# Decode samples' NSA on four column tiles of the PE array: compression, scores and value products re-laid

## The chip, the cores and the metric

The program runs on one core of a Trainium2 chip. A core has the matrix engine TensorE (PE in the profile; its weight loads are PEld), VectorE (DVE), ScalarE (ACT), GpSimd (POOL), and SyncE (SP), which here issues nearly all DMAs. They run side by side and wait for each other on semaphores. The metric is the device time of one execution in microseconds (us); lower is better.

## The reference, cut to what matters

The reference is one step of a hybrid decoder layer over a prompt of 1024 tokens and 8 decode samples with one new token each. The change is in the samples' NSA attention (`NS` = 8 samples, `NH` = 8 heads of `HD` = 64 in 2 kv groups, a cache of 1024 rows in 8 pages of 128):

```
kc, vc = compress(cached k, w_k), compress(cached v, w_v)   # blocks of 32 rows, weighted sum: 32 blocks per sample
p_c = softmax(q . kc);  o_c = p_c . vc                      # compressed branch
imp = sum of p_c over the group's 4 heads, pairs of blocks  # importance of 16 selection blocks of 64 rows
idx = top_k(imp, 16) of the 17 blocks (16 old, 1 new)       # so one old block is left out
o_s = softmax(q . k[idx]) . v[idx]                          # selected branch, 1024 rows
o_w = softmax(q . k_win) . v_win                            # window branch, 512 rows
out = g0 * o_c + g1 * o_s + g2 * o_w
```

Beside it the layer merges two mixers: `sigmoid(h W_a) * (ya W_pa) + sigmoid(h W_b) * (yb W_pb)` over 1032 tokens.

## The kernel before, in words

The program has long stages one after the other: adaLN, input projections, mLSTM, prompt attention, then the **merge stage** (from 850 to 1195 us of the trace), output rows, up projection, down projection. The samples' NSA has no stage of its own: it is laid into the merge stage. That stage has 24 units u. A unit of PE has one or two gate chains (8 f32 matmuls of 344 columns, stationary 128x128, line L2623), then the chains of ya and yb (4 matmuls each), eight together. Behind the gate chain stands `samples_pe(2u+1)`, behind the y chains `samples_pe(2u+2)`. `samples_dve` and `samples_act` have their calls at the same places on DVE and ACT. So the order on every engine is fixed in the code, by the number n = 2u+1 or 2u+2.

What stands there for sample b, before:

- n = 2b+3 (b = 0 to 7): first `scores` of sample b-1 (L2601 to L2603: the queries of all samples, zero but for one, as 64 stationary columns, against 1024 selected keys, 512 window keys and 32 compressed keys, accumulated over the samples in PSUM), then the transposes of b's 8 key pages (L2541), which DVE and ACT copy to SBUF.
- n = 2b+4: 4 transposes of the window keys (L2547), then compression: keys with the page stationary and 4 moving columns (L2554), values with a 32-column block pattern stationary (L2557). GpSimd must have multiplied the pages by the compression weights before (L1059), and does so as soon as all of b's keys are in.
- n = 19 to 24: softmax of the compressed branch, importance (L2562), mask, softmax of the others, transposes of the probabilities (L2566 to L2571).
- n = 25: products for the new row (L2575, L2576) and the compressed values (L2578), into one PSUM tile for all samples.
- n = 25 to 32: sample n-25's values: 12 pages stationary (128x128), 8 probabilities moving (L2585, L2588).
- n = 32: a closing matmul of zeros (L2592); DVE copies the result into ybT, which the unit u = 16 needs.

An f32 matmul stands twice in the trace (x16 is eight of the program).

**SP's queue** is one list, in this order: keys 0, merge weights 1, keys 1, merge weights 2, keys 2, keys 3, three outputs, merge weights 3, keys 4, keys 5, merge weights 4, keys 6, keys 7, merge weights 5, values 0 to 3, merge weights 6, merge weights 7, values 4 to 7, merge weights 8 and so on. One set of keys is 8 pages, for each a page number read from a table (L796), one DMA for the compressed rows (L798) and one for the selected keys (L800), then one for the window (L802). It goes into one of 2 slots and waits until the sample two before has been compressed. Values have 4 slots (L811 waits, L813 and L815 load); values 4 to 7 wait for the products of values 0 to 3. Merge weights (L835) have 2 slots; set m is for the units 2m and 2m+1 (m up to 7), and waits until the units of set m-2 are done.

Of the kernel before, what the change touches and what calls it, by code (L numbers as in the profile page):

```python
# [8 lines left out]
ALU = mybir.AluOpType  # L9
# [6 lines left out]
P = 128  # L16
# [4 lines left out]
NS = 8  # L21
# [40 lines left out]
def constants():  # L62
# [5 lines left out]
    parts["pick"] = (((np.arange(P)[:, None] % 32) == np.arange(16)[None, :]) & (np.arange(16)[None, :] < 9)) * 1.0  # L68
# [62 lines left out]
def build(nc, t, outs):  # L131
# [3 lines left out]
    with ExitStack() as ctx:  # L135
# [239 lines left out]
        vcs = take(NCMP, NS, NKV * HD)  # L375
        Qall, Qpad = take(P, NS, NH), take(P, NS, NH)
        knT = take(P, 2, NS)
        ckT = take(P, NCMP)
        assert at <= NT * MIX, at
        SR = NS * NH  # L380
        at = at_nsa
        pT, wT = take(P, PAST), take(P, WIN)
        PTs, PTw = pT[:, 0:512].unsqueeze(1), pT[:, 512:1024]
        Ssl, Swn = take(SR, PAST + NS), take(SR, WIN + NS)
# [19 lines left out]
        Scm, pcm = take(SR, NCMP), take(SR, NCMP)  # L404
# [98 lines left out]
        def up_lo(place, k):  # L503
# [36 lines left out]
        s_sps, s_Qall, s_soft, s_softm, s_softe, s_sPT, s_sPTe = (  # L540
            sem(n) for n in ("samples_ps", "Q_all", "soft", "soft_max", "soft_exp", "sPT_ps", "sPT"))
# [3 lines left out]
        SP_Q, SP_Y, SP_IMP, SP_O = 1, 2, 3, 4  # L545
# [561 lines left out]
        def _(act):  # L1107
# [136 lines left out]
            def samples_act(n):  # L1244
# [21 lines left out]
                if n == 19:  # L1266
                    for turn, x, j in ((1, Scm, 0), (2, Swn, 2)):
                        act.wait_ge(s_softm, turn)
                        nc.scalar.activation(x, x, ACT.Exp, bias=small[:, j:j + 1], accum_out=small[:, 4 + j:5 + j]).then_inc(s_softe, 1)
# [3 lines left out]
                if n == 24:  # L1273
                    act.wait_ge(s_sPT, 1)
                    nc.scalar.activation(PTs[:, 0, :], ps[:, 4, :], ACT.Copy).then_inc(s_sPTe, 1)

# [158 lines left out]
        def _(dve):  # L1435
# [356 lines left out]

            def samples_dve(n):
# [11 lines left out]
                if n == 1:  # L1805
# [6 lines left out]
                    dve.sem_inc(s_Qall, 1)  # L1812
# [19 lines left out]
                if 3 <= n <= 18 and n % 2 == 0:  # L1832
                    b = (n - 4) // 2
                    dve.wait_ge(s_pgps, 2 * b + 2)
                    nc.vector.tensor_copy(ckT, ps[:, 5, 0:NCMP])
                    nc.vector.tensor_copy(vcs[:, b, :], ps[0:NCMP, 5, 64:64 + P])
                    nc.vector.tensor_tensor(Qpad, Qall, cst("onehot")[:, b * NS:(b + 1) * NS].unsqueeze(2).to_broadcast([P, NS, NH]),
                                            ALU.mult).then_inc(s_pgd, 1)
# [32 lines left out]
                if n == 19:  # L1871
                    dve.wait_ge(s_soft, 1)
                    nc.vector.tensor_copy(Scm, ps[0:SR, 3, 64:64 + NCMP])
                    step(nc.vector.tensor_copy(Swn[:, 0:WIN], ps[0:SR, 2, :]))
# [3 lines left out]
                    nc.vector.tensor_reduce(small[:, 0:1], Scm, AX.X, ALU.max, negate=True).then_inc(s_softm, 1)  # L1878
                    nc.vector.tensor_reduce(small[:, 2:3], Swn, AX.X, ALU.max, negate=True).then_inc(s_softm, 1)
                    step(nc.vector.memset(zrow, 0.0))  # L1880
                if n == 20:
                    dve.wait_ge(s_softe, 1)
# [24 lines left out]
                if n == 24:  # L1907
                    dve.wait_ge(s_sPT, 1)
                    nc.vector.tensor_copy(PTw[:, 0:256], ps[:, 5, 0:256])
                    nc.vector.tensor_copy(PTw[0:NCMP, 256:320], ps[0:NCMP, 5, 256:320])  # L1910
                    nc.vector.tensor_copy(PTw[0:NS, 320:448], ps[0:NS, 5, 320:448]).then_inc(s_sPTe, 1)
                if n == 32:
                    dve.wait_ge(s_sps, SP_O)
# [256 lines left out]
        def _(pe):  # L2170
# [345 lines left out]
            def samples_pe(n):  # L2516
# [8 lines left out]
                if n == 3:  # L2525
                    pe.wait_ge(s_Qall, 1)
# [16 lines left out]
                if 3 <= n <= 18 and n % 2 == 0:  # L2543
# [16 lines left out]
                if n == 22:  # L2560
                    pe.wait_ge(s_soft, 2)
                    nc.tensor.matmul(ps[0:SR, 4, 0:NCMP], cst("same_group", SR), pcm, start=True, stop=True).then_inc(s_sps, 1)  # L2562
                if n == 24:
                    pe.wait_ge(s_soft, 3)
# [4 lines left out]
                    nc.tensor.transpose(ps[0:NCMP, 5, 256:320], Scm, ident[0:SR, 0:SR])  # L2569
                    nc.tensor.transpose(ps[0:NS, 5, 320:384], Ssl[:, PAST:], ident[0:SR, 0:SR])  # L2570
                    nc.tensor.transpose(ps[0:NS, 5, 384:448], Swn[:, WIN:], ident[0:SR, 0:SR]).then_inc(s_sPT, 1)  # L2571
                if n == 25:
# [4 lines left out]
                    for b in range(NS):  # L2577
                        nc.tensor.matmul(ps[:, 0, b * NH:(b + 1) * NH], vcs[:, b, :], PTw[0:NCMP, 256 + b * NH:256 + (b + 1) * NH],  # L2578
                                         start=False, stop=False, skip_group_check=True)
                if 25 <= n <= 32:  # L2580
                    b, v = n - 25, (n - 25) % 4
                    pe.wait_ge(*values_landed(b))
                    out = ps[:, 0, b * NH:(b + 1) * NH]
                    for j in range(NPAGE):
                        nc.tensor.matmul(out, pv_slc[v][:, j, :], PTs[:, 0, j * SR + b * NH:j * SR + (b + 1) * NH],  # L2585
                                         start=False, stop=False, skip_group_check=True)
                    for j in range(WIN // P):
                        ins = nc.tensor.matmul(out, pv_win[v][:, j, :], PTw[:, j * SR + b * NH:j * SR + (b + 1) * NH],  # L2588
                                               start=False, stop=False, skip_group_check=True)
                    ins.then_inc(s_free, 1)  # L2590
                if n == 32:
                    nc.tensor.matmul(ps[:, 0, 0:SR], ones[0:1, :], zrow[:, 0:SR], start=False, stop=True).then_inc(s_sps, 1)  # L2592

            def scores(b):

                first, last = b == 0, b == NS - 1
                pe.wait_ge(s_pga, 2 * b + 2)
                pe.wait_ge(s_pgd, 2 * b + 2)
                Q2 = Qpad.rearrange("p b h -> p (b h)")
# [204 lines left out]
```

## Time and profile before

| | us |
|---|---|
| median of 3 runs | 2087.64 |
| lowest, highest run | 2083.59, 2087.82 |
| span of the profiled execution (first to last instruction) | 2085.8 |
| PE busy in it | 2017.6 (97%) |
| DVE, ACT, POOL busy | 816.0, 517.7, 371.4 |
| mean granted TensorE clock | 0.983 |

The profiled execution has no time of its own beside its span; the median of the runs lies 1.84 us above that span. All places in the trace are in us from the span's start. A row of the timeline has the start, the length until the last of the group ends, engine, line, operation, tiles, shapes and how many. Matmuls overlap, so what a group costs is the distance from its start to the start of the row behind it, not its length.

### The profile page before, as it was taken

How to read it: one execution, taken by the hardware profiler on the slowest of the kernel's cores; microseconds unless marked ns; L12 is line 12 of the kernel's file. 1: busy time of each engine (PE TensorE's matmuls, PEld its weight loads, DVE VectorE, ACT ScalarE, POOL GpSimd, SP SyncE). 2: the span in 40 equal slices, each digit the busy share in tenths (PEclk: the TensorE clock that was granted, in tenths of full speed). 3: DMA queues.
4: the chain of work that ended last, by engine and by line, in shares of the span. 5: the costliest groups of instructions: out<-in, count | busy, mean ns of one | idle time of the engine just before them, and what ended most of it. 6: DMA issues, size and time to landing. Idle time of an engine off the chain costs nothing.

```text
span 2085.8 us, 28720 instructions
## 1 busy us (share of the span) xinstructions
PE 2017.6 (97%) x11391; PEld 1601.0 (77%) x11391; DVE 816.0 (39%) x1535; ACT 517.7 (25%) x942; POOL 371.4 (18%) x440
## 2 busy tenths in 40 slices
PE   6999999989999998999999999999999999999998
PEld 3589877775666665666676677999999999988876
DVE  2444333475656566622201257511211111235344
ACT  2322200133344444211200046411111111123232
POOL 0000111222222223222000043000000000145553
PEclk9999999989999999999989999999999999999999
DMA  9443001032000000454324355221121112235453
GB/s 362 142 152 102 21 30 34 1 90 81 11 11 11 11 11 11 135 159 139 104 81 110 87 180 179 62 62 41 41 59 43 41 44 58 91 121 169 144 192 112
DMA packets 172077, 184.38 MB, mean 88 GB/s; under 512 B 9925, under 2 KB 142253, under 8 KB 171502
## 3 DMA queue, kind: packets, MB, share of 16 engines
q1 hardware_dynamic: 171950, 182.59, 27.8%
q8 instruction: 91, 1.49, 0.3%
q14 instruction: 36, 0.29, 0.0%
HBM read 170.22 MB, written 16.53 MB: 90 GB/s over the span
## 4 chain that ended last, share of the span: by engine, by line
PE 89%; DVE 3%; DMA 2%; ACT 2%; issue 1%; SPq 1%; POOL 1%; ACTq 0%; POOLq 0%; DVEq 0%
PE ps L2722 23%; PE ps L2623 11%; PE ps L2226 8%; PE ps L2493 5%; PE ps L2665 5%; PE ps L2247 5%; PE ps L2667 5%; PE ps L2666 5%; PE ps L2444 3%; PE ps L2483 3%; PE ps L2461 3%; PE ps L2186 1%; PE ps L2557 1%; PE ps L2585 1%; PE ps L2601 1%
## 5 line engine op out<-in xcount | busy, mean ns | idle before, releaser
L2722 PE MATMUL ps<-h_hi,wup_hi 128*128 128x344 f32 x1008 | 322.4, 320 | 3.5 <-DVE arena L2076 3.5
L2722 PE MATMUL ps<-h_lo,wup_hi 128*128 128x344 f32 x1008 | 323.1, 321 | 0.0
L2722 PE MATMUL ps<-h_hi,wup_lo 128*128 128x344 f32 x1008 | 322.5, 320 | 0.0
L1082 POOL CAST ra_hi<-arena 128x384 fp32r<-128x384 f32 (+1 forms) x90 | 48.5, 539 | 848.2 <-PE ps L2722 453.1
L2226 PE MATMUL ps<-arena,hT 128*128 128x261 f32 (+2 forms) x768 | 193.5, 406 | 3.4 <-ACT hT L1137 2.5
L2665 PE MATMUL ps<-rw_hi,ra_hi 128*128 128x512 f32 x480 | 191.8, 400 | 5.1 <-DVE rw_lo L1924 5.1
L2722 PEld LDWEIGHTS ps<-h_hi,wup_hi 128*128 128x128 f32 x1008 | 189.5, 188 | 4.0 <-issue 2.6
L2722 PEld LDWEIGHTS ps<-h_lo,wup_hi 128*128 128x128 f32 x1008 | 189.6, 188 | 0.0
L2722 PEld LDWEIGHTS ps<-h_hi,wup_lo 128*128 128x128 f32 x1008 | 189.5, 188 | 0.0
L2667 PE MATMUL ps<-rw_lo,ra_hi 128*128 128x512 f32 x480 | 189.4, 395 | 0.0
L2666 PE MATMUL ps<-rw_hi,ra_lo 128*128 128x512 f32 x480 | 188.7, 393 | 0.0
L2226 PEld LDWEIGHTS ps<-arena,hT 128*128 128x128 f32 x768 | 143.1, 190 | 42.6 <-issue 7.4
L1051 POOL TENSOR_SCALAR arena<-arena 128x640 f32<-128x640 f32 (+7 forms) x128 | 99.9, 781 | 287.4 <-DVE arena L1774 287.4
L1924 DVE TENSOR_TENSOR rw_lo<-hT,rw_hi 128x1024 fp32r<-128x1024 f32 x65 | 90.1, 1391 | 143.6 <-ACT rw_hi L1281 143.6
L1214 ACT ACTIVATE arena<-ps,arena 128x640 f32<-128x640 f32 (+7 forms) x128 | 89.7, 700 | 186.8 <-DVE arena L1754 185.2
L2493 PE MATMUL ps<-hT,xn 128*128 128x344 f32 x336 | 128.0, 498 | 3.1 <-ACT arena L1238 2.4
L1088 POOL TENSOR_TENSOR ra_lo<-arena,ra_hi 128x384 fp32r<-128x384 f32 (+1 forms) x90 | 125.2, 1391 | 4.8
L2623 PE MATMUL ps<-hT,arena 128*128 128x344 f32 x400 | 123.2, 463 | 0.0
L2623 PE MATMUL ps<-arena 128*128 128x344 f32 x352 | 112.3, 474 | 0.7 <-ACT arena L1289 0.5
L2665 PEld LDWEIGHTS ps<-rw_hi,ra_hi 128*128 128x128 f32 x480 | 90.9, 189 | 28.2 <-issue 7.5
L1281 ACT ACTIVATE rw_hi<-hT 128x1024 fp32r<-128x1024 f32 x65 | 68.7, 1060 | 175.6 <-DMA hT<-in_w_down 175.6
L2667 PEld LDWEIGHTS ps<-rw_lo,ra_hi 128*128 128x128 f32 x480 | 90.8, 189 | 21.0
(429 smaller groups left out, 2923.9 us busy)
## 6 DMA issues: line engine op xcount, KB each, us to landing
hT<-in_w_down SPq DMA_DIRECT2D x65, 512.0 KB, 3.3
arena<-in_w_ada SPq DMA_DIRECT2D x12, 2048.0 KB, 8.1
arena<-in_w_up SPq DMA_DIRECT2D x42, 512.0 KB, 4.7
arena<-in_w_out SPq DMA_DIRECT2D x24, 512.0 KB, 4.1
arena<-in_w_in SPq DMA_DIRECT2D x17, 512.0 KB, 4.4
arena<-in_cache_cmp_kv SPq DMA_DIRECT2D x64, 128.0 KB, 2.0
arena<-in_cache_slc_kv SPq DMA_DIRECT2D x128, 64.0 KB, 1.9
arena<-in_w_in SPq DMA_DIRECT2D x4, 1544.0 KB, 12.9
```

What stands on the lines that cost most here:

```text
L1051: nc.gpsimd.tensor_scalar(pbuf[u % 3][:, 0:nb * P], pbuf[u % 3][:, 0:nb * P], rec[:, u % 4:u % 4 + 1], gts[:, i, col:col + 1], ALU.mult, A ...
L1088: nc.gpsimd.tensor_tensor(lo[:, 0:n], src[:, k, cols], hi[:, 0:n], ALU.subtract).then_inc(s_ra, 1)
L1214: nc.scalar.activation(pbuf[u % 3][:, 0:n], sp_[:, 512 - n // 2:512 + n // 2], ACT.Exp, bias=nmx[:, u % 4:u % 4 + 1], accum_out=rsum[:, u ...
L1924: nc.vector.tensor_tensor(rw_lo[rnd][at][:, :], rw_from(rnd, step), rw_hi[rnd][at][:, :], ALU.subtract).then_inc(s_rlo, 1)
L2226: ins = nc.tensor.matmul(ps[:, bank, 0:width], hT[:, k, n * P:(n + 1) * P], w[:, k, 0:width], start=(k == 0), stop=(k == KD - 1))
L2247: ins = nc.tensor.matmul(ps[:, mix_bank(j, n), 0:PA], h[:, k, :], w[:, k, :], start=(k == 0 and x == 0), stop=(k == KD - 1 and x == 2))
L2493: ins = nc.tensor.matmul(ps[:, 7, 0:TG], wfill[m % 2][:, k, :], hT[:, k, q * TG:(q + 1) * TG], start=(k == 0), stop=(k == KD - 1))
L2623: ins = nc.tensor.matmul(ps[:, bank, 0:TG], w[:, k, :], src[:, k, q * TG:(q + 1) * TG], start=(k == 0), stop=(k == kn - 1))
L2665: nc.tensor.matmul(out, ra_hi[rnd][a][:, rows], rw_hi[rnd][w][:, cols], start=first, stop=False)
L2666: nc.tensor.matmul(out, ra_lo[rnd][a][:, rows], rw_hi[rnd][w][:, cols], start=False, stop=False)
L2667: ins = nc.tensor.matmul(out, ra_hi[rnd][a][:, rows], rw_lo[rnd][w][:, cols], start=False, stop=last)
L2722: ins = nc.tensor.matmul(ps[:, bank, 0:TG], w(place, k0 + k), h[:, k, toks], start=(k == 0 and j == 0), stop=(k == KD - 1 and j == 2))
```

## The change

Compression (n = 2b+4): one matmul gives keys and values. The 32-column block pattern is stationary, and the weighted rows (128 keys, 128 values) are 256 moving columns. Page 2q+r goes to column tile q, that is PSUM partitions 32q to 32q+31; four samples accumulate in one PSUM region, which is copied once per four samples, and its key half transposed by PE (n = 12 and 19).

Scores: the stationary operand is the queries of four samples (32 columns), and the 1536 keys are four pieces of 384, one for each column tile, accumulated over four samples in PSUM bank b // 4. DVE and ACT bring them into the softmax layout (32 rows per four samples) at n = 13 and 19. Scores on compressed keys are one matmul for four samples (`cmp_scores`), with a mask for those of other samples (`cmp_masked`); the compressed softmax is now 64x128 instead of 64x32. DVE takes the block mask onto the copy in SBUF and not from PSUM.

Values: the probabilities of four samples (32 columns) are stationary, the pages of 128 columns move, page 4r+q in column tile q. At the end (new n = 33, behind the gate chain of u = 16) the result (2 copies of 128x512) is turned by 8 matmuls with the page sum `pick`, and added to the new row's and the compressed products. The wait of u = 16 for ybT moves from before both y chains to before the second.

```diff
@@ samples_pe
                 if 3 <= n <= 18 and n % 2 == 0:
...
-                    for j in range(NPAGE):
-                        nc.tensor.matmul(ps[:, 5, 4 * j:4 * j + 4], pg_cmp[s][:, j, 0:P], cst("block")[:, 28:32],
-                                         start=True, stop=True)
-                    for j in range(NPAGE):
-                        ins = nc.tensor.matmul(ps[0:NCMP, 5, 64:64 + P], cst("block")[:, 28 - 4 * j:60 - 4 * j],
-                                               pg_cmp[s][:, j, P:2 * P], start=(j == 0), stop=(j == NPAGE - 1))
+                    if b == 4:
+                        pe.wait_ge(s_qk, QK_CMP[0])
+                        nc.tensor.transpose(ps[:, 5, 0:P], kcv[0][:, 0:P], ident)
+                    if b == 5:
+                        cmp_scores(0, 5, P)
+                    for r in range(2):
+                        at = 8 * (b % 4) + 4 * r
+                        for q in range(4):
+                            ins = nc.tensor.matmul(ps[32 * q:32 * q + 32, 2, b // 4 * 256:b // 4 * 256 + 256],
+                                                   cst("block")[:, 28 - at:60 - at], pg_cmp[s][:, 2 * q + r, :],
+                                                   start=(b % 4 == 0 and r == 0), stop=(b % 4 == 3 and r == 1))
                     ins.then_inc(s_pgps, 1)
+                if n == 19:
+                    pe.wait_ge(s_qk, QK_CMP[1])
+                    nc.tensor.transpose(ps[:, 5, 0:P], kcv[1][:, 0:P], ident).then_inc(s_sps, 1)
+                if n == 20:
+                    pe.wait_ge(s_qk, QK_KT)
+                    cmp_scores(1, 4, 0).then_inc(s_sps, 1)
...
-                    for b in range(NS):
-                        nc.tensor.matmul(ps[:, 0, b * NH:(b + 1) * NH], vcs[:, b, :], PTw[0:NCMP, 256 + b * NH:256 + (b + 1) * NH],
+                    for g in range(2):
+                        nc.tensor.matmul(ps[:, 0, g * 32:(g + 1) * 32], kcv[g][:, P:2 * P], PTw[:, 256 + g * 32:256 + (g + 1) * 32],
                                          start=False, stop=False, skip_group_check=True)
                 if 25 <= n <= 32:
...
-                    for j in range(NPAGE):
-                        nc.tensor.matmul(out, pv_slc[v][:, j, :], PTs[:, 0, j * SR + b * NH:j * SR + (b + 1) * NH],
-                                         start=False, stop=False, skip_group_check=True)
-                    for j in range(WIN // P):
-                        ins = nc.tensor.matmul(out, pv_win[v][:, j, :], PTw[:, j * SR + b * NH:j * SR + (b + 1) * NH],
-                                               start=False, stop=False, skip_group_check=True)
+                    for r in range(3):
+                        for q in range(4):
+                            j = 4 * r + q
+                            w, v_ = (PTs[:, 0, :], pv_slc[v][:, j, :]) if r < 2 else (PTw, pv_win[v][:, q, :])
+                            at = (j if r < 2 else q) * SR + b // 4 * 32
+                            ins = nc.tensor.matmul(ps[32 * q:32 * q + 32, 1 + b // 4, b % 4 * P:(b % 4 + 1) * P], w[:, at:at + 32], v_,
+                                                   start=(r == 0), stop=(r == 2))
                     ins.then_inc(s_free, 1)
-                if n == 32:
+                if n == 33:
+                    pe.wait_ge(s_pga, 2 * NS + 2)
+                    pe.wait_ge(s_pgd, 2 * NS + 1)
+                    for b in range(NS):
+                        nc.tensor.matmul(ps[:, 0, b * NH:(b + 1) * NH], Obuf[:, b // 4, b % 4 * P:(b % 4 + 1) * P],
+                                         cst("pick")[:, b % 4 * NH:(b % 4 + 1) * NH], start=False, stop=False, skip_group_check=True)
@@ scores
-                for j in range(2):
-                    nc.tensor.matmul(ps[0:SR, j, :], Q2, pT[:, j * 512:(j + 1) * 512], start=first, stop=last)
-                nc.tensor.matmul(ps[0:SR, 2, :], Q2, wT, start=first, stop=last)
-                nc.tensor.matmul(ps[0:SR, 3, 64:64 + NCMP], Q2, ckT, start=first, stop=last).then_inc(s_free, 1)
+                for q in range(4):
+                    ins = nc.tensor.matmul(ps[32 * q:32 * q + 32, b // 4, 0:KCH], Qpad.rearrange("p b h -> p (b h)"),
+                                           KT[:, q * KCH:(q + 1) * KCH], start=(b % 4 == 0), stop=(b % 4 == 3))
+                ins.then_inc(s_free, 1)
@@ samples_dve, n == 22
-                    step(nc.vector.tensor_reduce(imp, ps[0:SR, 4, 0:NCMP].rearrange("p (k r) -> p k r", r=2), AX.X, ALU.add))
+                    step(nc.vector.tensor_reduce(pcm[:, 0:64], ps[0:SR, 4, 0:P].rearrange("p (k r) -> p k r", r=2), AX.X, ALU.add))
+                    step(nc.vector.tensor_reduce(imp.rearrange("p (q k) -> p q k", q=4),
+                                                 pcm[:, 0:64].rearrange("p (q b k) -> p q k b", q=4, b=4), AX.X, ALU.add))
...
-                    for j in range(2):
-                        ins = nc.vector.tensor_tensor(Ssl[:, j * 512:(j + 1) * 512].rearrange("p (k c) -> p k c", c=SEL),
-                                                      ps[0:SR, j, :].rearrange("p (k c) -> p k c", c=SEL),
-                                                      msk[:, j * 8:(j + 1) * 8].unsqueeze(2).to_broadcast([SR, 8, SEL]), ALU.add)
-                    step(ins)
+                    S3 = Ssl[:, 0:PAST].rearrange("p (k c) -> p k c", c=SEL)
+                    step(nc.vector.tensor_tensor(S3, S3, msk.unsqueeze(2).to_broadcast([SR, 16, SEL]), ALU.add))
```

On PE, one sample's part of the merge stage before, from its scores to the gate chain behind its successor's compression (each row: line of its kernel, operation, tiles, output partitions x columns, how many):

```order
L2601 MATMUL ps<-arena 64x512 x2
L2602 MATMUL ps<-arena 64x512
L2603 MATMUL ps<-arena 64x32
L2541 MATMUL ps<-const,arena 128x128 x8
L2623 MATMUL ps<-arena 128x344 x8
L2547 MATMUL ps<-const,arena 128x128 x4
L2554 MATMUL ps<-const,arena 128x4 x8
L2557 MATMUL ps<-arena,const 32x128 x8
L2623 MATMUL ps<-hT,arena 128x344 x8
```

The same stretch on PE in the changed kernel:

```order
L2654 MATMUL ps<-arena 32x384 x4
L2579 MATMUL ps<-const,arena 128x128 x8
L2678 MATMUL ps<-arena 128x344 x8
L2585 MATMUL ps<-const,arena 128x128 x4
L2600 MATMUL ps<-arena,const 32x256 x8
L2678 MATMUL ps<-hT,arena 128x344 x8
```

Four score matmuls became four of 32 partitions, and the sixteen of the compression eight; chains and transposes stand where they stood.

On PE, n = 25 and the first two samples' values before:

```order
L2575 MATMUL ps<-arena 128x64
L2576 MATMUL ps<-arena 128x64
L2578 MATMUL ps<-arena 128x8 x8
L2585 MATMUL ps<-arena 128x8 x8
L2588 MATMUL ps<-arena 128x8 x4
L2623 MATMUL ps<-arena 128x344 x8
L2585 MATMUL ps<-arena 128x8 x8
L2588 MATMUL ps<-arena 128x8 x4
```

And in the changed kernel:

```order
L2625 MATMUL ps<-arena 128x64
L2626 MATMUL ps<-arena 128x64
L2628 MATMUL ps<-arena 128x32 x2
L2638 MATMUL ps<-arena 32x128 x12
L2678 MATMUL ps<-arena 128x344 x8
L2638 MATMUL ps<-arena 32x128 x12
```

The count per sample stays twelve, with 128 moving columns in place of 8 and a quarter of the output partitions. The instructions of SP and GpSimd are the same in both kernels, in the same order.

## Rows read from the trace of the kernel before

**Rows 1.** Value part: length, busy of PE, PEld, DVE, ACT, POOL, clock, DMA share.

```profile
1033.40:1114.20 80.80, 80.80 (x377) 60.82 (x375) 7.07 (x16) 3.88 (x7) 0.00 (x0) 0.87 0.29 76
```

**Rows 2.** Waits of PE, 850 to 1200 us: total, times, longest.

```profile
PE ps L2541 <- DMA arena<-in_cache_win_kv: 1.2, 1, 1.2
```

**Rows 3.** Timeline of PE, one sample's cycle of the key part.

```profile
953.07 1.93 PE L2601 MATMUL ps<-arena 128*64 128x512 f32 x4
...
955.88 1.09 PE L2541 MATMUL ps<-const,arena 128*128 128x128 f32 x8
...
961.88 1.85 PE L2554 MATMUL ps<-const,arena 128*128 128x4 f32 x16
963.65 1.94 PE L2557 MATMUL ps<-arena,const 128*32 128x128 f32 x16
965.52 4.89 PE L2623 MATMUL ps<-hT,arena 128*128 128x344 f32 x16
970.34 1.07 PE L2601 MATMUL ps<-arena 128*64 128x512 f32 x2
```

**Rows 4.** Timeline of PE, matmuls with 32 stationary columns on four column tiles.

```profile
30.48 1.92 PE L2186 MATMUL ps<-arena 128*32 128x512 f32 x16
...
132.29 1.50 PE L2232 MATMUL ps<-arena,hT 128*32 128x386 f32 x16
133.73 0.44 PE L2247 MATMUL ps<-mw_hi,mh_hi 128*128 128x386 f32 x1
```

**Rows 5.** Timeline of POOL: it starts when a sample's keys have landed.

```profile
867.08 4.68 POOL L1059 TENSOR_TENSOR arena<-arena 128x1024 f32<-128x1024 f32 x2 [20.65 <-DMA arena<-in_cache_win_kv]
883.21 4.68 POOL L1059 TENSOR_TENSOR arena<-arena 128x1024 f32<-128x1024 f32 x2 [11.44 <-DMA arena<-in_cache_win_kv]
...
932.30 4.66 POOL L1059 TENSOR_TENSOR arena<-arena 128x1024 f32<-128x1024 f32 x2 [14.68 <-DMA arena<-in_cache_win_kv]
...
982.87 4.66 POOL L1059 TENSOR_TENSOR arena<-arena 128x1024 f32<-128x1024 f32 x2 [13.39 <-DMA arena<-in_cache_win_kv]
```

**Rows 6.** Timeline of SP's queue: one set of keys, its first and last issue.

```profile
949.06 0.36 SPq L798 DMA_DIRECT2D arena<-in_cache_cmp_kv  x1
...
961.99 0.43 SPq L802 DMA_DIRECT2D arena<-in_cache_win_kv  x1
```

**Rows 7.** Waits of SP's queue for the samples, 850 to 1020 us.

```profile
SPq L796 <- PE ps L2557: 6.1, 3, 3.2
SPq L811 <- PE ps L2557: 1.0, 1, 1.0
```

**Rows 8.** Timeline of SP: values 0's first issue, and merge weights 6.

```profile
983.60 8.16 SPq L813 DMA_DIRECT2D arena<-in_cache_slc_kv  x8
...
1021.62 0.50 SPq L835 DMA_DIRECT2D arena<-in_w_in  x1
...
1022.79 0.51 SPq L835 DMA_DIRECT2D arena<-in_w_proj_b  x1
```

**Rows 9.** DMA issues by line: count, KB each, us to landing.

```profile
arena<-in_w_proj_b SPq DMA_DIRECT2D x15, 256.0 KB, 5.2
```

**Rows 10.** Timeline of PE, value part.

```profile
1033.46 4.89 PE L2623 MATMUL ps<-hT,arena 128*128 128x344 f32 x16
1038.28 0.43 PE L2575 MATMUL ps<-arena 8*128 8x64 f32 x2
...
1040.60 3.16 PE L2585 MATMUL ps<-arena 128*128 128x8 f32 x16
...
1060.31 1.85 PE L2585 MATMUL ps<-arena 128*128 128x8 f32 x16
...
1062.91 4.87 PE L2623 MATMUL ps<-arena 128*128 128x344 f32 x16
```

**Rows 11.** Windows in the value part, columns as in rows 1.

```profile
1041.20:1051.20 10.00, 10.00 (x31) 7.64 (x31) 0.51 (x1) 0.00 (x0) 0.00 (x0) 0.50 0.09 26
1082.10:1085.40 3.30, 3.30 (x8) 2.12 (x8) 0.00 (x0) 0.00 (x0) 0.00 (x0) 0.50 0.22 64
```

More of the change, by code:

```diff
@@ L374, in build @@
         at = 21568
-        vcs = take(NCMP, NS, NKV * HD)
-        Qall, Qpad = take(P, NS, NH), take(P, NS, NH)
+        kcv = [take(P, 2 * NKV * HD) for _ in range(2)]
+        ckT = [take(P, P) for _ in range(2)]
+        SR = NS * NH
+        Scm, pcm = take(SR, P), take(SR, P)
+        Qall, Qpad = take(P, NS, NH), take(P, 4, NH)
         knT = take(P, 2, NS)
-        ckT = take(P, NCMP)
         assert at <= NT * MIX, at
-        SR = NS * NH
         at = at_nsa
-        pT, wT = take(P, PAST), take(P, WIN)
+        KCH = (PAST + WIN) // 4
+        KT = take(P, PAST + WIN)
+        pT, wT = KT[:, 0:PAST], KT[:, PAST:]
         PTs, PTw = pT[:, 0:512].unsqueeze(1), pT[:, 512:1024]
+        Obuf = room(at, 2, 4 * P)
         Ssl, Swn = take(SR, PAST + NS), take(SR, WIN + NS)
@@ L1265, in samples_act @@
                     nc.scalar.activation(hg[:, 9:10], hg[:, 9:10], ACT.Sqrt).then_inc(s_shd, 1)
[L1266 to L1269, printed above, removed]
+                if n in (13, 19):
+                    g = int(n == 19)
+                    act.wait_ge(s_free, 4 * g + 4)
+                    for q in range(2):
+                        ins = nc.scalar.activation(Ssl[32 * g:32 * g + 32, q * KCH:(q + 1) * KCH], ps[32 * q:32 * q + 32, g, 0:KCH], ACT.Copy)
+                    if g:
+                        ins.then_inc(s_pga, 1)
+                if n in (19, 20):
+                    turn, x, j = ((1, Swn, 2), (2, Scm, 0))[n - 19]
+                    act.wait_ge(s_softm, turn)
+                    nc.scalar.activation(x, x, ACT.Exp, bias=small[:, j:j + 1], accum_out=small[:, 4 + j:5 + j]).then_inc(s_softe, 1)
                 if n == 22:
@@ L1275, in samples_act @@
                     nc.scalar.activation(PTs[:, 0, :], ps[:, 4, :], ACT.Copy).then_inc(s_sPTe, 1)
+                if n == 32:
+                    act.wait_ge(s_free, NS + 4)
+                    nc.scalar.activation(Obuf[:, 0, :], ps[:, 1, :], ACT.Copy).then_inc(s_pga, 1)
             def rows_hi(rnd, step):
@@ L1790, in _, with cmp_masked @@
                     att_max(n + 2)
+            def cmp_masked(g, bank, at):
+                rows = slice(32 * g, 32 * g + 32)
+                own = cst("own_new")[rows, 4 * g:4 * g + 4].unsqueeze(1).unsqueeze(3).to_broadcast([32, 4, 4, 8])
+                return nc.vector.tensor_tensor(Scm[rows, :].rearrange("p (q b c) -> p q b c", q=4, b=4),
+                                               ps[rows, bank, at:at + P].rearrange("p (q b c) -> p q b c", q=4, b=4), own, ALU.add)
             def samples_dve(n):
@@ L1877, in samples_dve @@
                     step(nc.vector.memset(Swn[:, 0:1], NEG))
-                    nc.vector.tensor_reduce(small[:, 0:1], Scm, AX.X, ALU.max, negate=True).then_inc(s_softm, 1)
                     nc.vector.tensor_reduce(small[:, 2:3], Swn, AX.X, ALU.max, negate=True).then_inc(s_softm, 1)
+                    dve.wait_ge(s_sps, SP_KT)
+                    nc.vector.tensor_copy(ckT[1], ps[:, 5, 0:P]).then_inc(s_qk, 1)
                     step(nc.vector.memset(zrow, 0.0))
                 if n == 20:
-                    dve.wait_ge(s_softe, 1)
+                    dve.wait_ge(s_sps, SP_CMP)
+                    step(cmp_masked(1, 4, 0))
+                    nc.vector.tensor_reduce(small[:, 0:1], Scm, AX.X, ALU.max, negate=True).then_inc(s_softm, 1)
+                if n == 21:
+                    dve.wait_ge(s_softe, 2)
                     step(nc.vector.reciprocal(small[:, 8:9], small[:, 4:5]))
@@ L2604, in scores, with cmp_scores @@
-                if last:
-                    pe.wait_ge(s_free, NS)
-                    pe.sem_inc(s_soft, 1)
+                for q in range(4):
+                    ins = nc.tensor.matmul(ps[32 * q:32 * q + 32, b // 4, 0:KCH], Qpad.rearrange("p b h -> p (b h)"),
+                                           KT[:, q * KCH:(q + 1) * KCH], start=(b % 4 == 0), stop=(b % 4 == 3))
+                ins.then_inc(s_free, 1)
+            def cmp_scores(g, bank, at):
+                return nc.tensor.matmul(ps[32 * g:32 * g + 32, bank, at:at + P], Qall[:, 4 * g:4 * g + 4, :].rearrange("p b h -> p (b h)"),
+                                        ckT[g], start=True, stop=True)
```

61 lines of the change are left out of this document (35 added, 26 removed).

## Prediction

> **What bounds the kernel now.** I read the page first: PE is busy 97% of the span and the chain of waits is 89% PE, so PE's time counts wherever it does not wait. The samples' NSA lies between 865 and 1114 us. The list of PE's waits there has one wait for data, 1.2 us for the first keys [rows 2]; the timeline shows everything else back to back. So now each microsecond of the samples' matmuls is paid in full. The second view is SP's queue and the landing of its loads, because a shorter PE can ask for data sooner than SP brings it. I think that this view decides the size.
>
> **What PE alone would save.** Distances between starts, in the steady cycle of one sample [rows 3], 17.27 us long: scores 953.07 to 955.88, 2.81 us; compression 961.88 to 965.52, 3.64; the rest (two chains, twelve transposes) 10.8.
> What 32 columns on four column tiles cost, the trace shows in another stage: sixteen matmuls of 512 columns show 1.92 us together, and four of 512 on one tile show 1.93 [rows 3, 4]. So four tiles run side by side, 0.43 us for a group of four. Sixteen of 386 columns take 1.44 us to the next start (132.29 to 133.73 [rows 4]), four groups of 0.32 and some 0.12 to change back. For changing into such a group I put 0.09 more, an estimate a little under the 0.12 of changing back; before scores the kernel already changes (to 64 columns), so it counts only for compression and values. This gives:
> - scores, 8 of 384 columns: 2 x 0.32 + 0.12 = 0.76, saves 2.05;
> - compression, 16 of 256 columns: 4 x 0.22 + 0.12 + 0.09 = 1.09, saves 2.55;
> - so a cycle of 17.27 - 4.60 = 12.67 us;
> - values: now 1060.31 to 1062.91, 2.60 us per sample [rows 10]. New: 24 of 128 columns in 6 groups. The nearest row is L2557, also 32 stationary and 128 moving but on one tile: 1.87 us for 16, 0.117 each [rows 3]. Side by side 6 x 0.117 + 0.2 = 0.90, saves 1.70, x 8 = 13.6. One after the other it would be 24 x 0.117 + 0.2 = 3.0, a loss of 0.4. I take the first, because rows 4 are the same four tiles.
>
> A rule of the Trainium skill speaks against this: in "TensorE: Matmul & The Clock Gate", Part 3 (packing small matmuls), weight loads overlap running matmuls only when the row group differs, and column tiles share it. By that each group would pay a load of some 0.11 us too, 6 x 0.11 x 8 = 5.3 us for the values, and the time would be 2059. Rows 4 disagree: 0.43 us per group is just the streaming of 512 columns and leaves no room for a load.
>
> **The keys: SP takes most of it back.** One set of keys takes 12.9 us from first to last issue [rows 6], some 0.8 us for the page number of the next set stands between, and every second set has three DMAs of merge weights behind it, about 1.7 us. So SP needs some 14.5 us per sample on average, against PE's new 12.67. How much of SP's time before was waiting for PE? In the whole key part 6.1 us, three times, and none before keys 5 [rows 7]. So the landings of keys 0 to 4 do not move at all, and those of keys 7 move by at most 6.1. POOL shows the landings: 867.08, 883.21, 932.30 (keys 4), 982.87 (keys 7) [rows 5]. After: PE would be ready for keys 1 at 880.2 (867.08, a cycle, and 0.4 for a small mLSTM product) and gets them at 883.2; it gets keys 4 at 932.3; keys 7 at 982.87 - 6.1 = 976.8. Before, PE took keys 7 at 973.15 + 17.27 = 990.4. PE alone would have come there at 956.2, so 20 of its microseconds turn into waits of 1 to 6 us ahead of the transposes. From the transposes to the start of compression it is 6.00 us (955.88 to 961.88 [rows 3]), with compression 7.1: the last compression ends at 983.9 instead of 1000.05. GpSimd's 4.68 us from landing [rows 5] are within the 6.0 us before compression needs them, so they stay hidden. Behind the waiting transposes stand the y chains, and nobody but DVE and ACT waits for those.
>
> **n = 19 to 24.** Scores of sample 7 save 2.05. Added on PE: one transpose 0.11, `cmp_scores` 0.33 and 0.09, importance with 128 columns 0.11. Then PE waits 0.5 us for ACT, whose exp ends a chain over DVE's n = 22; there one more reduce and the mask from SBUF add about 0.25. PE could begin unit 12, which began at 1033.46 [rows 10], at 1015.9.
> But unit 12 needs merge weights 6, and SP issues these behind values 0 to 3: 983.60 to 1021.62, 38.0 us [rows 8]. Ahead of it all, SP can win what it waited, 6.1 + 1.0 [rows 7]: first issue at 1014.5, the last of the three 1.2 later [rows 8], landed 5.2 later [rows 9], at 1020.9. So unit 12 starts 12.6 us earlier than before, not 17.6, and PE stands 5 us idle. I add 1.7 us for the clock, which falls after such a wait (one half-clock stretch of 3.3 us costs half its length).
>
> **Values.** From 1033.46 to the closing matmul took 80.4 us at a mean clock of 0.87 [rows 1]. 10 us at 0.50, and three stretches of 3.3 at 0.50 [rows 11], which has one of the three, cost half of 20, 10.2. Each follows the start of weight-bound matmuls of 8 columns (the first at 1038.28 to 1045.3 [rows 10]): PE loads, but moves little. After, no such group is left but the closing one: the values stream 128 columns on all tiles. I take it that all 10.2 come back; the bound is none. n = 25: 2.32 us before [rows 10], after 0.27 + 0.22 + 4 x 0.11 = 0.94, saves 1.4. New n = 33: 16 matmuls of 8 columns at 0.11 is 1.8 us on the path; copies by ACT and DVE for it lie beside the gate chain, and ybT's copies beside the ya chain, which no longer waits.
> SP: values 4 wait for the products of values 0 (about 1029.5), then 9.4 us a sample, the last ones at 1067; PE needs them at 1055 and 1077. Covered, with 7 us of room.
> Sum: 80.4 - 10.2 - 13.6 - 1.4 + 1.8 + 1.7 = 58.7 instead of 80.4, 21.7 us.
> **Total:** 12.6 + 21.7 = 34.3 us. Everything after (units 16 on, rows, up and down projection) is ordered by PE and moves as a block; I give it nothing. Against the execution's own span 2085.8 - 34.3 = 2051.5; the median of the runs lies 1.84 above the span, so 2053.4.
>
> **Range of this case.** No clock won back: +10. Weights of unit 12 landing at 1019 or 1023, issues that take 1.3 us instead of 0.4 (several such in each stretch of SP): 3 us either way. Half-clock after each wait for keys: mostly hidden, since PE waits for the next keys anyway, up to +3. So 2046 to 2066.
>
> **Rivals.**
> 1. *PE sets the pace, SP does not bind.* All of 8 x 4.60, 1.7 for a half-clock stretch at 928, and 23.4 of the value part (21.7 without the new clock loss), less 0.8: 61 us, 2026. For it: DMA engines are far from full. Against it: the issue time is SP's own and does not shrink. 4%.
> 2. *The short matmuls do not run side by side* (the change does less than it says). Scores 2.66, compression 3.66, values 3.0: cycle -0.13, values +0.4 x 8 = 3.2, n = 25 and 33 even, clock not won back: +2 us, 2089, within measurement. Against it rows 4; for it only that no row has 128 moving columns on four tiles. 5%.
> 3. *Slower: the waits keep PE's clock at its lower level (1.2 GHz) through the key part.* A dense PE that now waits 1 to 6 us in each cycle could run its chains at half speed: cycle 25.3, last compression at 867 + 8 x 25.3 + 0.4 = 1070, 70 later than before, the rest saves 24: 2133. The skill's same page (its section on clock oscillation) says that bursts parted by idle gaps fall back to the lower clock. The trace shows half-clock for single stretches, not for a stage. It turns slower only when over 100 of the 247 us are at half clock (half of them lost, against 34 won and 20 of waits as cushion). 4%.
> 4. *A wait I don't see, at the merge weights or a copy of DVE beside GpSimd*, smaller than the gain: 2066 to 2083. 8%.
>
> **Chances.** My forecast 79%. What a measurement of this kernel can tell from no change is 0.2%, 4 us. Faster by more 93%, within 3%, slower 4%. The range of eight in ten: 2044 to 2067.
>
> **What would show it.** PE waits on the window-key DMA ahead of the transposes in most cycles, some 20 us in total; POOL's starts at 932.3 and near 976.8; PE's cycle is 12.7 us where it does not wait; SP's waits of 6.1 are gone; unit 12 waits some 5 us for L835; groups of twelve value matmuls take 0.9 us to the next start; the value part has a clock near 1. Wrong would be: POOL's starts moved well ahead of these, a group of values above 2 us, or a clock below 0.9 in the keys.

## The result and the profile after

The changed kernel takes 2049.59 us in the median of 4 runs (2047.03 to 2054.07), the one before 2086.74 beside it (4 runs): ratio 0.9829, 95% interval 0.9814 to 0.9845, that is 37 us less where 34 were forecast. The profiled execution has a span of 2045.2 us against 2085.8. A second set of runs gave 2047.36 against 2083.26, ratio 0.9828 (0.9814 to 0.9841).

The page after, busy time and chain by engine. Before, PE was busy 97% of the span and had 89% of the chain; SP's queue had 1%.

```profile
PE 1960.5 (96%) x11273; PEld 1548.0 (76%) x11273; DVE 811.3 (40%) x1529; ACT 520.3 (25%) x947; POOL 372.9 (18%) x440
...
PE 82%; SPq 7%; DVE 3%; issue 3%; ACT 2%; DMA 2%; POOL 1%; ACTq 0%; POOLq 0%; DVEq 0%
```

In this one row the bound has moved: 7% of the chain now runs through SP's issues. Where PE waits, 850 to 1200 us (total, times, longest), against the single 1.2 of [rows 2]:

```profile
PE ps L2579 <- DMA arena<-in_cache_win_kv: 11.4, 7, 5.2
PE ps L2678 <- DMA arena<-in_w_proj_b: 6.3, 1, 6.3
```

SP's waits of [rows 7] are gone: it waits for nothing between 850 and 1020 us. POOL's starts show the landing of keys 0, 1, 4 and 7, answering to [rows 5]:

```profile
864.66 4.68 POOL L1063 TENSOR_TENSOR arena<-arena 128x1024 f32<-128x1024 f32 x2 [20.53 <-DMA arena<-in_cache_win_kv]
880.63 4.66 POOL L1063 TENSOR_TENSOR arena<-arena 128x1024 f32<-128x1024 f32 x2 [11.29 <-DMA arena<-in_cache_win_kv]
...
927.31 4.66 POOL L1063 TENSOR_TENSOR arena<-arena 128x1024 f32<-128x1024 f32 x2 [13.45 <-DMA arena<-in_cache_win_kv]
...
969.72 4.68 POOL L1063 TENSOR_TENSOR arena<-arena 128x1024 f32<-128x1024 f32 x2 [8.67 <-DMA arena<-in_cache_win_kv]
```

The whole stage began 2.3 us earlier in this execution (unit 0 at 848.38, before at 850.68), so places are compared from there: keys 4 at 81.6 before and 78.9 after, keys 7 at 132.2 and 121.3.

PE's timeline, first a wait for keys 4 and what follows it, then one sample's cycle (answering to [rows 3]):

```profile
927.29 1.97 PE L2579 MATMUL ps<-const,arena 128*128 128x128 f32 x8 [5.20 <-DMA arena<-in_cache_win_kv]
929.05 6.75 PE L2678 MATMUL ps<-arena 128*128 128x344 f32 x16
...
954.99 0.85 PE L2654 MATMUL ps<-arena 128*32 128x384 f32 x8
956.36 1.09 PE L2579 MATMUL ps<-const,arena 128*128 128x128 f32 x8 [0.51 <-DMA arena<-in_cache_win_kv]
957.29 4.79 PE L2678 MATMUL ps<-arena 128*128 128x344 f32 x16
961.92 0.60 PE L2585 MATMUL ps<-const,arena 128*128 128x128 f32 x4
962.45 1.07 PE L2600 MATMUL ps<-arena,const 128*32 128x256 f32 x16
963.45 4.89 PE L2678 MATMUL ps<-hT,arena 128*128 128x344 f32 x16
```

Compression takes 1.00 us to the next start (962.45 to 963.45) and took 3.64; scores, where no wait follows (942.10 to 942.88), take 0.78 and took 2.81. The y chains behind the long wait need 6.75 us instead of 4.79: the mean granted clock from 926 to 936 us is 0.66. Then unit 12 and the values, answering to [rows 10]:

```profile
1015.27 6.39 PE L2678 MATMUL ps<-hT,arena 128*128 128x344 f32 x16 [6.29 <-DMA arena<-in_w_proj_b]
1021.59 0.43 PE L2625 MATMUL ps<-arena 8*128 8x64 f32 x2
...
1022.74 0.86 PE L2638 MATMUL ps<-arena 128*32 128x128 f32 x24
1023.53 4.89 PE L2678 MATMUL ps<-arena 128*128 128x344 f32 x16
...
1076.83 1.85 PE L2645 MATMUL ps<-const,arena 128*128 128x8 f32 x16
1078.61 0.43 PE L2647 MATMUL ps<-arena,ones 1*128 1x64 f32 x2
1078.97 6.30 PE L2678 MATMUL ps<-arena 128*128 128x344 f32 x15
```

A sample's twelve products take 0.79 us to the next start (1022.74 to 1023.53), before 2.60. Windows of the value part and of what follows the closing turn, columns as in [rows 1]:

```profile
1015.20:1078.90 63.70, 63.63 (x394) 41.54 (x394) 6.77 (x13) 4.32 (x8) 0.00 (x0) 0.98 0.35 97
1080.00:1083.00 3.00, 3.00 (x7) 1.72 (x6) 0.45 (x3) 0.00 (x0) 2.23 (x4) 0.50 0.50 119
```

The mean granted clock is 0.98 where it was 0.87. One half-clock stretch (0.50) follows the sixteen matmuls of 8 columns that are left, at 1080, and the y chains behind them take 6.59 us in all. This stretch does not come every time: in the trace of the second set of runs the same chains take 4.89.

```profile
1078.02 1.85 PE L2645 MATMUL ps<-const,arena 128*128 128x8 f32 x16
...
1080.15 4.89 PE L2678 MATMUL ps<-arena 128*128 128x344 f32 x16
```

### The profile page after: what moved, and what is told of

Same layout as the page of the kernel before. It is cut to its first block, busy times and chain, and to the rows that moved or that the text cites. A ratio compares the mean times of both kernels' runs of the same rounds, so it can differ in the third digit from the quotient of the medians.

```text
span 2045.2 us, 28485 instructions
## 1 busy us (share of the span) xinstructions
PE 1960.5 (96%) x11273; PEld 1548.0 (76%) x11273; DVE 811.3 (40%) x1529; ACT 520.3 (25%) x947; POOL 372.9 (18%) x440
## 4 chain that ended last, share of the span: by engine, by line
PE 82%; SPq 7%; DVE 3%; issue 3%; ACT 2%; DMA 2%; POOL 1%; ACTq 0%; POOLq 0%; DVEq 0%
PE ps L2776 24%; PE ps L2264 9%; PE ps L2678 6%; PE ps L2531 5%; PE ps L2285 5%; PE ps L2719 5%; PE ps L2721 5%; PE ps L2720 5%; PE ps L2482 3%; PE ps L2521 3%; PE ps L2499 3%; SPq L800 1%; SPq L804 1%; SPq L802 1%; DMA arena<-in_w_ada 1%
## 5 line engine op out<-in xcount | busy, mean ns | idle before, releaser
L2678 PEld LDWEIGHTS ps<-hT,arena 128*128 128x128 f32 x400 | 75.5, 192 | 48.4 <-DMA arena<-in_w_proj_b 6.5
```

Source lines behind the costliest of these rows:

```text
L2678: ins = nc.tensor.matmul(ps[:, bank, 0:TG], w[:, k, :], src[:, k, q * TG:(q + 1) * TG], start=(k == 0), stop=(k == kn - 1))
```

## Experiments

Ratios are to the kernel before, timed on the same chip; the changed kernel's is 0.983. In the sums of the expectations SP and PE are as in the prediction.

**1. No page lookup.** Is SP's issue what paces the keys?

```
-  page = sp.value_load(ptab[0:1, b * NPAGE + j:...], min_val=0, max_val=...)
+  page = b * NPAGE + j
```

> The changed kernel, but SP takes page b*8+j as a constant and reads no page number from the table (it leaves out the lookup; the pages read are others, of the same size). This frees about 0.77 us of SP's 1.57 us per page pair in the keys and 0.7 per page in the values. Theory (SP's issue time sets the pace of the keys, and merge weights 6 come late behind it): PE's waits for keys (11.4 us) and for the weights of unit 12 (6.3 us) vanish, and with them the half-clock stretches behind them (some 3 us); a cycle is 12.7 us throughout; about 2029 us, 20 below the changed kernel. Rival (the DMA engines or the landing itself set the pace, and SP only looks busy): landings move by 2 us at most in all, PE still waits about 10 us; 2045 to 2048.

Measured: 2021.65 us, ratio 0.9712 (0.9689 to 0.9735), some 24 us below the changed kernel by the ratios (20 were expected). PE has no wait for a load left. SP, in the same window as [rows 7], now waits for PE:

```profile
SPq L837 <- PE ps L2676: 26.3, 5, 18.9
SPq L801 <- PE ps L2598: 11.0, 4, 4.6
```

PE over 100 us of the key part (windows, as above):

```profile
860.00:960.00 100.00, 100.00 (x540) 61.76 (x538) 55.77 (x75) 16.83 (x28) 41.64 (x16) 1.00 0.74 204
```

PE is busy 100%, at clock 1.00, while the DMA engines move 204 GB/s; the changed kernel's 864 to 984 us show 0.62 and 169 GB/s. So the engines had room, and it was the issuing that held the keys back. The 24 us are more than PE's waits of 17.7 (11.4 + 6.3): the half-clock stretches behind the waits, some 6 us by the rows of the changed kernel, go as well.

SP's timeline, from page to page of a constant number, 0.95 us:

```profile
940.53 0.43 SPq L801 DMA_DIRECT2D arena<-in_cache_cmp_kv  x1
941.00 0.43 SPq L803 DMA_DIRECT2D arena<-in_cache_slc_kv  x1
941.48 0.43 SPq L801 DMA_DIRECT2D arena<-in_cache_cmp_kv  x1
```

**2. Merge weights 6 earlier.** Only that wait is taken away.

```
-  for b in range(4): load_values(b)
-  load_merge(6)
+  load_values(0); load_values(1)
+  load_merge(6)
+  load_values(2); load_values(3)
```

> The changed kernel with merge weights 6 ahead of values 2 in SP's queue instead of behind values 3. Theory (unit 12 stands only on the place of that load in the queue): the 6.3 us wait of PE goes, with some 1.5 us of half clock behind it; values 2 and 3 land 1.8 us later and have 5 us to spare; 2042 us. Rival 1 (the slot of these weights is free too late, or values 2 and 3 become the wait): half of it, 2046. Rival 2 (unit 12 would wait for the softmax chain anyway): no change, 2049.

Measured: 2038.08, ratio 0.9791 (0.9770 to 0.9812), 8 us less than the changed kernel by the ratios (7.6 were expected); the interval leaves anything from 3 to 12 us. The wait for w_proj_b is gone, and that for keys is as it was:

```profile
PE ps L2581 <- DMA arena<-in_cache_win_kv: 11.6, 6, 4.6
```

So the wait of unit 12 is SP's order, not the bandwidth. In the two traces the stage, from its unit 0 to the first output row, takes 301.4 us instead of 308.7, 7.4 less: the 6.3 us of the wait and the clock behind it account for that.

**3. The values in their old form** in the changed kernel (keys, scores and compression changed; values with 8 moving columns; no n = 33).

```
-  nc.tensor.matmul(ps[32*q:32*q+32, 1+b//4, ...], w[:, at:at+32], v_, ...)
+  nc.tensor.matmul(ps[:, 0, b*NH:(b+1)*NH], pv_slc[v][:, j, :], PTs[:, 0, j*SR+b*NH:...], ...)
```

> The changed kernel with the value products in their old form (page stationary, 8 probabilities moving, straight into the one result; no closing turn, no copies for it). Theory (the new form saves 1.8 us of PE per sample, and the half clock of the old value part came from its weight-bound matmuls): 8 x 1.8 = 14.4 back, 1.8 and 1.5 for the closing turn and the half-clock stretch behind it saved, and three or four half-clock stretches of 1.7 us return or the long one does, 5 to 10 us; together 2066 to 2072. Rival (the clock stretches had to do with something else in the old value part): PE's time alone, 2060 to 2062.

Measured: 2063.84, ratio 0.9914 (0.9892 to 0.9936): 17.7 us slower than the changed kernel, by the ratios. That is 2067 on the scale of the expectation, its low end. The half clock is back behind four of the eight groups of products. One of them, timeline and window:

```profile
1027.67 1.85 PE L2629 MATMUL ps<-arena 128*128 128x8 f32 x16
...
1030.27 6.57 PE L2667 MATMUL ps<-hT,arena 128*128 128x344 f32 x16
```

```profile
1031.30:1034.00 2.70, 2.70 (x6) 1.64 (x5) 0.00 (x0) 0.00 (x0) 0.00 (x0) 0.50 0.36 105
```

The key part alone is then worth 18 us (0.9914 of 2082 to 2087), the value part the other 18. A longer stretch at half clock (1007 to 1017 us of that trace) is not of the products' making: it lies in the wait for merge weights 6 (6.2 us) and in the chain behind it, ahead of the first product, as in the changed kernel.

**4. The value products on one tile.** All twelve go to column tile 0, so the sums over the other tiles are left out; eight transposes fill the other partitions once, at n = 25.

```
-  ps[32*q:32*q+32, ...], start=(r == 0), stop=(r == 2)
+  ps[0:32, ...], start=(r == 0 and q == 0), stop=(r == 2 and q == 3)
```

> The changed kernel with all twelve value matmuls of a sample on column tile 0 (output partitions 0 to 31), same operands and sizes; eight transposes of 0.11 us fill the other partitions first. It leaves out the right sum. Theory (the gain of the new form is that four tiles run side by side): 24 x 0.117 + 0.2 = 3.0 us per sample instead of 0.8, 8 x 2.2 + 0.9 = 18.5 us more, 2068; with half clock in the value part, if what the PE moves per time counts, up to 2078. Rival (the tiles did not run side by side, it is the shape that is cheap): 2050 to 2051.

Measured: 2063.52, ratio 0.9906 (0.9883 to 0.9928), 16 us slower than the changed kernel by the ratios (18.5 were expected). Timeline and window:

```profile
1038.68 2.81 PE L2640 MATMUL ps<-arena 128*32 128x128 f32 x24
1041.41 4.89 PE L2680 MATMUL ps<-arena 128*128 128x344 f32 x16
```

```profile
1023.50:1093.00 69.50, 69.50 (x354) 50.15 (x354) 6.86 (x13) 3.22 (x6) 0.00 (x0) 1.00 0.27 76
```

A group takes 2.73 us instead of 0.79; eight times the difference is 15.5 us, and with the 0.9 us of the transposes that is all of what was lost. Four tiles are worth a factor of 3.5 here. The clock stays at 1.00 here and fell to 0.50 behind half of the groups in experiment 3: the low clock goes with products of 8 moving columns behind 128-column loads, not with one tile working alone.

**5. Column-tiled compression and scores done twice.** PE gets 12.1 us more work in the key part (compression 1.00 to 1.86 us, scores 0.78 to 1.43, for eight samples). If PE's time counted there, it would show in full. The chip is that of the second set of runs above.

```
-  for r in range(2):                              # compression; scores likewise
+  for rep, r in ((0, 0), (0, 1), (1, 0), (1, 1)):
```

> The changed kernel with the column-tiled compression and scores done twice in a row for every sample (sums are doubled, so the attention's values are others). PE gets 0.9 + 0.7 = 1.6 us more per sample, 13 us in all. Theory (SP's queue sets the pace of the keys, and unit 12 waits for merge weights 6 behind it): most of it lies in waits that are there anyway; PE's waits for keys shrink from 11.4 to about 5 us, the 6.3 us wait of unit 12 to 1 to 3 us, and the time rises by 0 to 3 us. Rival (PE's own time counts in full here as well): 13 us more.

Measured: 2046.91, ratio 0.9819 (0.9803 to 0.9834), against 2047.36 for the changed kernel beside it: nothing, and the 13 us of the rival are far outside the interval. PE's waits are now:

```profile
PE ps L2579 <- DMA arena<-in_cache_win_kv: 7.1, 5, 3.6
PE ps L2678 <- DMA arena<-in_w_proj_b: 1.9, 1, 1.9
```

In the profile beside it the changed kernel has 13.2 and 6.3, 19.5 in all, so 10.5 of the 12.1 go into them. The rest is paid by the clock: behind the shorter waits there is less of it at half, for instance the gate chain of unit 12 takes 4.89 us here and 7.62 in the trace beside it, and the mean clock from 864 to 984 us is 0.99 instead of 0.96. This is the clearest proof of the prediction's main step: with SP as it is, 12 us of PE's work more in the key part cost no time that can be measured.

**6. Weights early, and no bounds check on the page number.** The lookup stays, but SP no longer tests that the number lies in the pool.

```
+  page = nc.values_load(ptab[...], engines=[SP], ..., skip_runtime_bounds_check_because=...)
```

> Merge weights 6 ahead of values 2, and the page numbers read without the runtime bounds check (two sequencer instructions fewer per page, 0.27 us of 1.57). SP's time per set of keys falls from 12.5 to 10.4 us, with merge weights to about 11.7 on average, under PE's 12.67. Theory: PE's waits for keys fall from 11.5 to 1 to 3 us; 18 us below the changed kernel, ratio to the kernel before 0.974. Rival (the landing or the DMA engines set the pace, beyond SP's issue): as the early weights alone, 0.979.

Measured: 2025.58, ratio 0.9725 (0.9710 to 0.9740); again 2026.69, 0.9717 (0.9694 to 0.9740):

> Early weights and no bounds check, on the same chip as the run with the outputs later, for a direct comparison: ratio to the kernel before 0.9725 again, within 0.0015.

That is 22 us below the changed kernel (18 were expected). One page's pair of issues, SP's timeline of this kernel and of the changed one:

```profile
940.85 0.33 SPq L803 DMA_DIRECT2D arena<-in_cache_cmp_kv  x1
941.28 0.38 SPq L805 DMA_DIRECT2D arena<-in_cache_slc_kv  x1
942.14 0.33 SPq L803 DMA_DIRECT2D arena<-in_cache_cmp_kv  x1
```

```profile
913.28 0.34 SPq L802 DMA_DIRECT2D arena<-in_cache_cmp_kv  x1
913.72 0.38 SPq L804 DMA_DIRECT2D arena<-in_cache_slc_kv  x1
914.85 0.34 SPq L802 DMA_DIRECT2D arena<-in_cache_cmp_kv  x1
915.29 1.09 SPq L804 DMA_DIRECT2D arena<-in_cache_slc_kv  x1
```

1.29 us from pair to pair against 1.57. The DMA issues themselves take the same 0.33 and 0.38; the check is the 0.28 between them, 2.2 us per sample. PE keeps one wait, for keys 4, of 2.2 us here and 3.5 in the repeat. Where it does not wait, its cycle from transposes to transposes is 12.70 us:

```profile
873.97 1.09 PE L2583 MATMUL ps<-const,arena 128*128 128x128 f32 x8
...
886.67 1.09 PE L2583 MATMUL ps<-const,arena 128*128 128x128 f32 x8
```

**7. The merge weights on ACT's queue.** Sets 3 to 7 are issued by ACT at units 4, 6, 8, 10 and 12; no bounds check.

> Merge weights 3 to 7 issued by ScalarE right behind the gate sigmoid of units 4, 6, 8, 10 and 12 instead of by SP, and page numbers without the bounds check. SP has only keys and values, 11.2 us per sample. Theory: PE waits for nothing in the keys but the first ones, 20 us below the changed kernel, ratio 0.9735; ScalarE has 1.7 us more per two units, in gaps. Rival (ScalarE's issues hold up its copies and sigmoids, which PE waits for): above the kernel with early weights and no bounds check by 2 us or more.

Measured: 2027.51, ratio 0.9728 (0.9713 to 0.9743). The number came as expected, "no wait" did not: 3.9 us for keys 4 are left. The kernel of 6 is 2 us faster by the medians and level by the ratios, so the rival is not shown. Two queues are no better here than one in the right order, since after 6 only one wait is to be had.

**8. The same two SP edits in the kernel before.**

> The kernel before (old PE work) with the two edits of SP's queue that brought the changed kernel down by 22 us: no bounds check on page numbers, merge weights 6 ahead of values 2. Theory (SP's queue matters only since the change, because before it PE's work covered it): PE's one wait for data in the stage, 1.2 us for the first keys, goes, nothing else; ratio to the kernel before 0.999 to 1.000. Rival (the two edits are worth the same in any kernel, 22 us): 0.990.

Measured: 2084.28, ratio 0.9992 (0.9980 to 1.0003), 2 us by the ratio, which may be nothing. PE's 1.2 us wait is gone. SP now waits, from 850 to 1020 us, 21.0 us for the compression and 20.5 for the merge units:

```profile
SPq L796 <- PE ps L2561: 21.0, 5, 6.0
SPq L837 <- PE ps L2627: 20.5, 4, 15.8
```

Edits worth 22 us behind the change are worth 4 us at most ahead of it: the bound of the key part moved from PE to SP.

**9. The mLSTM outputs later.** As 6, and the three output DMAs that stand between keys 3 and keys 4 go behind merge weights 4.

```
   load_keys(4); load_keys(5); load_merge(4)
+  sp.wait_ge(s_sCn, 1); rows(C_sample ...); rows(n_sample ...); rows(m_sample ...)
```

> Early weights and no bounds check as before, and the three outputs of the samples' mLSTM state (2.2 us of SP ahead of merge weights 3 and keys 4) moved behind merge weights 4. Theory: the one wait for keys that is left (2.2 us, at keys 4) goes, and with it the half-clock stretch of 1.7 us that follows; some 3.5 us below the kernel with the two edits, ratio to the kernel before 0.971. Rival (the wait moves to keys 5 or 6, since the outputs still take their time): 1 us or less.

Measured: 2022.91, ratio 0.9695 (0.9674 to 0.9716), 3.8 us below its neighbour, with intervals that overlap, though each of its five runs is faster than each of the neighbour's five. Windows 915 to 935 us of this one and of the repeat of 6:

```profile
915.00:935.00 20.00, 20.00 (x118) 12.63 (x114) 5.81 (x13) 3.66 (x7) 8.21 (x4) 1.00 0.79 208
```

```profile
915.00:935.00 20.00, 16.48 (x83) 9.61 (x82) 2.63 (x6) 2.29 (x4) 8.47 (x4) 0.91 0.71 200
```

The wait and the clock loss behind it are gone from PE there; one wait of 1.0 us is left, two samples later, with no loss of clock behind it. By the ratio it is the fastest of all kernels run here, 64 us (3%) below the one before.

The repeat of the changed kernel that stood beside 5 to 7 had this expectation:

> The changed kernel itself, on the same chip as the next three, so that they can be compared with it directly. Both theories: its ratio to the kernel before is 0.983 again, within 0.002.

## Why the prediction was right, step by step

- **PE alone.** Cycle 12.67 forecast, 12.70 measured (experiment 6). Scores took 0.78 us (0.76 forecast), compression 1.00 (1.09). Reading the cost of four tiles from two rows of another stage [rows 4] was enough.
- **SP takes most of it back: right, and shown.** Experiments 1, 5 and 8 say it in three ways. The mis-sized term is "those of keys 7 move by at most 6.1": they came 10.9 us earlier from the start of the stage (132.2 to 121.3). SP's own waits of 6.1 went as forecast; the remaining 4.8 are shorter issues. Issues of 0.3 to 0.5 us now and then take 1.0 to 1.6, and there were fewer of those in the after trace (in the first set behind the three outputs one, 1.09 us, where before two, 1.30 and 1.27). Up to the last key load there were six among the loads of keys before and three after, which is 3.9 us. I had treated SP's issue time as fixed. Why they are rarer was not tried; the other traces with the same order and edits of SP up to there (the repeat and experiments 2 to 5) have one to three, so their number varies from execution to execution, and there is one trace of the kernel before. I count these 4 us as luck, not as an effect of the change.
- **PE's waits.** "Some 20 us in total": 11.4 in seven, and in the other profile 13.2. The 20 were the distance of keys 7 from where PE alone would have come. That distance is 15.8 us (121.3 from the start of the stage, where PE alone was to come at 105.5): less by the same 4.8. Of the 15.8, 10.3 are waits (the seven without the first), some 4.5 are half clock behind them, which I had put at next to nothing because it would be hidden. It is hidden, but in place of waiting; the last 1 us is small work on PE.
- **Unit 12.** "12.6 us earlier": 15.9 earlier from the start of the stage (182.8 to 166.9), again by SP's shorter time, so the 3.3 us above the forecast are luck for the greater part. The wait for merge weights 6 is 6.3 us, 5 were forecast.
- **Value part.** 80.4 to 58.7 forecast, a gain of 21.7. To the y chains of unit 16, the first work that is the same again, it went from 85.5 us (1033.46 to 1118.93) to 63.7 (1015.27 to 1078.97): 21.8. Inside it errors cancel: a group takes 0.79 us and not 0.90 (0.9 us more gained over eight), n = 25 takes 1.15 and not 0.94, n = 33 with what follows 2.14 and not 1.8.
- **Clock.** "All 10.2 come back" held up to the closing turn (the stretches listed cost 9.95 us, so 10.2 is a little high); behind its sixteen matmuls of 8 columns at 1076.83 stands one new stretch at 1080, 1.7 us (the units from there to the output rows took 76.36 us, after 78.16). I had written of that group and left it out of the sum. The other traces bear the sum out: ten traces have the same closing turn, and in eight of them the chain behind it takes 4.89 us; only here and in experiment 2 does it take 6.6.
- **A rule that failed.** The Trainium skill, "TensorE: Matmul & The Clock Gate", Part 3, has weight loads overlap only when the row group differs. The trace does not agree: by my estimate six groups would pay 6 x 0.11 us for loads and 6 x 0.117 for streaming, 1.4 us, and the twelve products take 0.79. The 2059 that this gave did not come. In experiment 4, on one tile, the same matmuls take 2.73.
- **The rest.** From unit 0 to the first output row the stage went from 344.6 us to 308.7, 35.9 less, which is 15.9 + 21.8 - 1.8. The two profiled executions differ by 40.6, 4.7 more: 2.3 ahead of the stage and 2.4 behind it, where the code does the same. The medians differ by only 37, so I take most of the 4.7 for the spread between executions; no run isolates it. That the forecast of 34 came within 3 us rests in part on such errors cancelling.

Rival 1 (PE sets the pace, 61 us less) did not happen, but it is about what the kernel becomes when SP's delays go: 60 us less in experiment 1, 57 in 6 and 64 in 9, by the ratios. Rival 2 (short matmuls not side by side) falls with the 0.79 us. Rival 3 (clock low through the key part) was wrong in size, not in kind: the mean clock of 864 to 984 us is 0.96, with single half-clock stretches there behind the waits, at about 882 and from 926 on, and one at the wait of unit 12. Rival 4's unseen wait did not appear.

## What to carry over

When matmuls get shorter on the engine that sets the pace, read next how long the queue behind its loads takes by itself, per round, waits left out: here 14.5 us of issuing against a new cycle of 12.7 decided that more than half of the saving in the key part was lost (some 36 us of PE's work, 15.9 us of time). Then test an issue cost where it counts: the same edits gave 2 us or nothing before the change and 22 us after it. To know whether an engine still binds, double its suspect work, and read its waits and its clock beside the time. And before a stretch of low clock is put down to the work in front of it, look for the same work in the other traces: the stretch behind the closing turn is missing in eight of ten.

## What I had not expected of the hardware

- A page number read from a table costs SP almost as much as the two DMAs that use it: 1.57 us per page, with a constant number 0.95 (experiment 1), so 0.62 for the lookup, of which the bounds check is 0.28. The two issues are 0.72 (0.34 + 0.38); with a constant number they stand back to back and take 0.43 each.
- Twelve f32 matmuls (24 in the trace) of 32 stationary and 128 moving columns take 0.79 us on four column tiles and 2.73 on one, so even at 128 columns the tiles run side by side with their weight loads.
- Those on one tile leave the clock at 1.00, though they take as long as the old 128-stationary, 8-moving form (2.60 us), behind which it falls to 0.50 at four of eight places, in the kernel before and in experiment 3.
- A wait of 5.2 us ahead of dense work costs more than itself: the next sixteen matmuls took 6.75 us instead of 4.79. Behind a wait of 2.72 us in the same trace they took 6.48, but behind 2.65 us in experiment 4 they took 4.79.
